# A streaming encoder step: the sample's convolution taps as ScalarE products, summed in groups on VectorE

## The reference

```
u      = ga_in * sigmoid(gb_in)                       # GLU, 512 channels
u_full = concatenate([past_conv, u])                  # 30 frames of history in front, zeros for the prompt
c      = depthwise causal convolution of u_full, 31 taps, one weight per channel and tap
c      = silu(layernorm(c + conv_dw_b))
conv_out = c @ w_conv_out
x = x + (sigmoid(ga) * attn_out + sigmoid(gc) * conv_out) @ w_out
```

## Time and profile before

| what | value |
|---|---|
| median of 3 runs | 1997.33 us (1996.92 to 1998.19) |
| profiled execution | 1996.86 us, span 1995.1 us |
| PE busy in the span | 1872.1 us (94%) |
| DVE busy | 1094.6 us (55%) |
| ACT busy | 766.1 us (38%) |
| POOL busy | 261.0 us (13%) |
| mean granted PE clock | 0.979 of full speed |

### The profile page before, as it was taken

How to read it: one execution, slowest core, us unless ns; L and a number is a source line. 1 busy time by engine, 2 the same in 40 slices (tenths; PEclk the granted TensorE clock), 3 DMA queues, 4 the chain that set the end, 5 groups by cost and what they waited for, 6 DMA issues and landing times.

```text
span 1995.1 us, 28433 instructions
## 1 busy us (share of the span) xinstructions
PE 1872.1 (94%) x11088; PEld 1647.4 (83%) x11088; DVE 1094.6 (55%) x1712; ACT 766.1 (38%) x1471; POOL 261.0 (13%) x287
## 2 busy tenths in 40 slices
PE   6977999999989966988999999999999999999998
PEld 3533799899989944656988889999999999999997
DVE  1045799897988977776454343333443333433333
ACT  2235655622367147765122233333223333333321
POOL 1001122122296022330000000000000000000000
PEclk9988999999999988999999999999999999999999
DMA  7110110332121323775321133333433333433332
GB/s 210 17 54 18 46 43 27 107 102 91 62 66 44 99 89 109 267 249 215 137 111 43 32 147 126 127 125 124 162 114 122 121 122 123 157 125 126 126 126 105
DMA packets 74236, 220.28 MB, mean 110 GB/s; under 512 B 14197, under 2 KB 25109, under 8 KB 65315
## 3 DMA queue, kind: packets, MB, share of 16 engines
q1 hardware_dynamic: 67963, 205.05, 30.3%
q10 hardware_dynamic: 6192, 14.16, 1.8%
HBM read 197.26 MB, written 21.89 MB: 110 GB/s over the span
## 4 chain that ended last, share of the span: by engine, by line
PE 56%; ACT 2%; DVE 1%; issue 1%; DVEq 0%; ACTq 0%
PE ps L653 17%; PE ps L652 17%; PE ps L651 17%; PE ps L881 1%; PE ps L858 1%; ACT buf L1260 1%; PE ps L915 1%; PE ps L900 1%; PE ps L871 1%; DVE buf L1571 1%; PE ps L971 0%; PE ps L887 0%; DVE buf L1396 0%; ACT buf L1250 0%; ACT buf L1302 0%
## 5 line engine op out<-in xcount | busy, mean ns | idle before, releaser
L651 PE MATMUL ps<-buf,buf 128*128 128x384 f32 (+2 forms) x2364 | 830.7, 351 | 17.3 <-DVE buf L1396 11.7
L653 PE MATMUL ps<-buf,buf 128*128 128x384 f32 (+2 forms) x2364 | 832.6, 352 | 0.0
L652 PE MATMUL ps<-buf,buf 128*128 128x384 f32 (+2 forms) x2364 | 830.7, 351 | 0.0
L651 PEld LDWEIGHTS ps<-buf,buf 128*128 128x128 f32 x2364 | 446.6, 189 | 43.2 <-DVE buf L1396 10.0
L652 PEld LDWEIGHTS ps<-buf,buf 128*128 128x128 f32 x2364 | 446.5, 189 | 24.3
L653 PEld LDWEIGHTS ps<-buf,buf 128*128 128x128 f32 x2364 | 446.2, 189 | 24.3
L1396 DVE TENSOR_TENSOR buf<-buf,buf 128x1024 fp32r<-128x1024 f32 (+4 forms) x245 | 335.6, 1376 | 184.2 <-ACT buf L1374 39.1
L1744 DVE TENSOR_TENSOR buf<-buf,ps 128x384 f32<-128x384 f32 x66 | 36.5, 553 | 403.1 <-PE ps L653 403.1
L1519 DVE SCALAR_TENSOR_TENSOR buf<-buf,buf,buf 128x1024 f32<-128x1024 f32 x240 | 197.4, 864 | 4.0
L1372 ACT ACTIVATE buf<-ps 128x384 f32<-128x384 f32 x66 | 32.5, 492 | 295.9 <-PE ps L653 295.9
L1374 ACT ACTIVATE buf<-buf 128x384 fp32r<-128x384 f32 x66 | 34.7, 525 | 282.1 <-DVE buf L1744 282.1
(11 more groups left out here) (182 smaller groups left out, 1746.5 us busy)
## 6 DMA issues: line engine op xcount, KB each, us to landing
buf<-in_w_ffn SPq DMA_DIRECT2D x67, 1024.0 KB, 5.6
buf<-in_w_ffn SPq DMA_DIRECT2D x66, 512.0 KB, 3.6
buf<-in_cache_k SPq DMA_DIRECT2D x16, 1024.0 KB, 7.3
buf<-in_cache_v SPq DMA_DIRECT2D x16, 1024.0 KB, 10.5
buf<-in_w_cols SPq DMA_DIRECT2D x24, 512.0 KB, 4.1
buf<-in_x SPq DMA_DIRECT2D x18, 512.0 KB, 3.7
gate_scr<-buf ACTq DMA_DIRECT2D x16, 576.0 KB, 4.8
buf<-gate_scr SPq DMA_DIRECT2D x16, 576.0 KB, 5.2
```

The source lines that it names most:

```text
L651: mm(dst, whi, xhi, start=start, stop=False)
L652: mm(dst, whi, xlo, start=False, stop=False)
L653: return mm(dst, wlo, xhi, start=False, stop=stop)
```

## The change

The prompt's part of a tap stays on DVE. The sample's part becomes a product alone, made by ACT into a buffer `prod` of two halves with six slots each, in the free bytes at `o_gmix`: group n of tile j holds 6 taps (the first group, with the bias in tap 0) or 5, six groups per tile, 24 in all. DVE adds up each group with one reduction over the slots (`sample_sum`, reading slot after slot, 128 floats apart) and adds that to the running sum of the tile; the last add of a tile goes straight to `cT`. ACT makes groups 0 to 5 behind named evacuations of the gate columns, groups 6 to 20 at the end of named turns of the head loop, the last three behind it. ACT waits until the half it writes has been summed; DVE waits until the group it sums is made.

The order of DVE's stream is written anew: after every tap a group sum where the tap's number is 8, 13, ... 118, the `qkv_low` behind taps 20, 50, 66, 82, 98 and 114, the memset behind 118, the last group sum at the end. The copy to `cT` takes the prompt's 1024 columns alone. PE's `layer_sums` also waits for the 24 sums. Two semaphores are merged into others (`biasS_in` into `near_in`, `rik_made` into `rstd_made`), and SP no longer waits for `conv_made` in front of `qkv_in(3)`.

```diff
+        prod = take(12 * P, o_gmix).rearrange("p (e d t) -> p e d t", e=2, d=6)
+        cuts = (0, 6, 11, 16, 21, 26, CK)
+        NPART = len(cuts) - 1
...
             qkv_in(2)
-            sp.wait_ge(S("conv_made"), 2)
             sp.wait_ge(S("out_state"), 48)
...
                     pe.wait_ge(S("conv_made"), CT)
+                    pe.wait_ge(S("sample_summed"), CT * NPART)
...
+            def sample_products(n):
+
+                j, i = divmod(n, NPART)
+                if n >= 2:
+                    act.wait_ge(S("sample_summed"), n - 1)
+                else:
+                    act.wait_ge(S("mask_made"), NSEL)
+                for d in range(cuts[i], cuts[i + 1]):
+                    out = prod[:, n % 2, d - cuts[i]].rearrange("p (s q) -> p s q", s=NS)
+                    x = uSamp[:, j, :, d:d + QS]
+                    if d:
+                        l = ac(out, x, ACT.Copy, scale=cw[:, j, d:d + 1])
+                    else:
+                        l = ac(out, x, ACT.Identity, scale=cw[:, j, d:d + 1], bias=cb[:, j:j + 1])
+                    l.then_inc(S("sample_made"), 1)
+
+            in_columns = {(20, 2): 0, (21, 1): 1, (21, 2): 2, (22, 2): 3, (23, 1): 4, (23, 2): 5}
+            in_heads = {13 * k // 5: 6 + k for k in range(15)}
...
                     l.then_inc(S("col_evac"), 1)
+                    if (t, c) in in_columns:
+                        sample_products(in_columns[t, c])
...
                     qkv_high(q // NT + 1)
+                if q in in_heads:
+                    sample_products(in_heads[q])
             qkv_high(5)
+            for n in range(6 + len(in_heads), CT * NPART):
+                sample_products(n)
...
             def conv_tap(j, d):
 
-                outs = (acc[:, 0:NP], acc[:, NP:NTOK].rearrange("p (s q) -> p s q", s=NS))
-                w = cw[:, j, d:d + 1]
-                for x, out in ((uT[:, j, d:d + NP], outs[0]), (uSamp[:, j, :, d:d + QS], outs[1])):
-                    if d == 0:
-                        ch.add(ve.tensor_scalar(out, x, w, cb[:, j:j + 1], ALU.mult, ALU.add))
-                    else:
-                        ch.add(ve.scalar_tensor_tensor(out, x, w, out, ALU.mult, ALU.add))
-                ch.wait()
+                x, w, out = uT[:, j, d:d + NP], cw[:, j, d:d + 1], acc[:, 0:NP]
+                if d == 0:
+                    ch.link(ve.tensor_scalar(out, x, w, cb[:, j:j + 1], ALU.mult, ALU.add))
+                else:
+                    ch.link(ve.scalar_tensor_tensor(out, x, w, out, ALU.mult, ALU.add))
                 if d == CK - 1:
-                    ve.tensor_copy(cT[:, j], acc).then_inc(S("conv_made"), 1)
+                    ve.tensor_copy(cT[:, j, 0:NP], out).then_inc(S("conv_made"), 1)
                     dve.wait_ge(S("conv_made"), j + 1)
 
+            def sample_sum(n):
+
+                j, i = divmod(n, NPART)
+                dve.wait_ge(S("sample_made"), j * CK + cuts[i + 1])
+                src = prod[:, n % 2, 0:cuts[i + 1] - cuts[i]].rearrange("p d t -> p t d")
+                total, part = acc[:, NP:NTOK], newneg
+                if n:
+                    dve.wait_ge(S("sample_summed"), n)
+                if i == 0:
+                    l = ve.tensor_reduce(total, src, AX.X, ALU.add)
+                else:
+                    ch.link(ve.tensor_reduce(part, src, AX.X, ALU.add))
+                    dst = cT[:, j, NP:NTOK] if i == NPART - 1 else total
+                    l = ve.tensor_tensor(dst, total, part, ALU.add)
+                l.then_inc(S("sample_summed"), 1)
...
-            convolve(20)
-            qkv_low(0)
-            convolve(20)
-            for f in range(1, 6):
-                qkv_low(f)
-                convolve(14)
-            dve.wait_ge(S("qn_made"), 2 * NT)
-            dve.wait_ge(S("turn_made"), NQK)
-            ve.memset(biasS, 0.0).then_inc(S("biasS_zero"), 1)
-            convolve(CT * CK)
+            sums = iter(range(CT * NPART))
+            low_behind = {20: 0, 50: 1, 66: 2, 82: 3, 98: 4, 114: 5}
+            for m, (j, d) in enumerate(all_taps, 1):
+                conv_tap(j, d)
+                if m >= 8 and m % 5 == 3 and m < 123:
+                    sample_sum(next(sums))
+                if m in low_behind:
+                    qkv_low(low_behind[m])
+                if m == 118:
+                    dve.wait_ge(S("qn_made"), 2 * NT)
+                    dve.wait_ge(S("turn_made"), NQK)
+                    ve.memset(biasS, 0.0).then_inc(S("biasS_zero"), 1)
+            for n in sums:
+                sample_sum(n)
```

More of the change, by code:

```diff
@@ L527, in _ @@
                 r = slice(h * QS, (h + 1) * QS)
-                sp.dma_start(biasS[r, PAST - P:PAST], skewed(h)[0:QS, 0:P]).then_inc(S("biasS_in"), 16)
+                sp.dma_start(biasS[r, PAST - P:PAST], skewed(h)[0:QS, 0:P]).then_inc(S("near_in"), 16)
                 sp.dma_start(biasS[r, PAST:LS].rearrange("p (s q) -> p s q", s=NS),
                              skewed(h)[0:QS, P:P + QS].unsqueeze(1).to_broadcast([QS, NS, QS]))\
-                    .then_inc(S("biasS_in"), 16)
+                    .then_inc(S("near_in"), 16)
             def keys_in(st_):
@@ L1422, in _ @@
             ve.tensor_reduce(ssq[:, 0:NT], ikn[:, :, 0:HD], AX.X, ALU.add).then_inc(S("ssik_made"), 1)
-            dve.wait_ge(S("rik_made"), 1)
+            dve.wait_ge(S("rstd_made"), NT + 1)
             ch.link(ve.tensor_tensor(ikwN[:, :, 0:HD], ikwN[:, :, 0:HD],
@@ L1706, in normed @@
             def normed(t):
-                dve.wait_ge(S("rstd_made"), NT + t + 1)
+                dve.wait_ge(S("rstd_made"), NT + t + 2)
                 ve.scalar_tensor_tensor(xs[:, t % 2], x1[:, t], rstd[:, t % 3:t % 3 + 1], gmix, ALU.mult, ALU.mult)\
@@ L1801, in _ @@
             ch.link(gp.tensor_scalar(msq[:, 0:NT], ssq[:, 0:NT], 1.0 / HD, EPS, ALU.mult, ALU.add))
-            gp.tensor_tensor(rsq[:, 0:NT], msq[:, 0:NT], mhalf[:, 0:NT], ALU.pow).then_inc(S("rik_made"), 1)
+            gp.tensor_tensor(rsq[:, 0:NT], msq[:, 0:NT], mhalf[:, 0:NT], ALU.pow).then_inc(S("rstd_made"), 1)
             for b in range(2, PB):
@@ L1859, in _ @@
             pool.wait_ge(S("qkv_done"), NQ)
-            pool.wait_ge(S("near_in"), 16 * H)
-            pool.wait_ge(S("biasS_in"), 16 * 2 * H)
+            pool.wait_ge(S("near_in"), 16 * 3 * H)
             for i in range(len(steps)):
```

## The result

The changed kernel takes 2008.55 us (median of 4 runs, 2007.56 to 2008.69) against 1997.12 for the kernel before beside it (1995.99 to 1998.19): ratio 1.0056, 95% interval 1.0039 to 1.0074. It is slower, by some 11 us. The forecast was 1996.3, no change; the time lies inside its range of 1988 to 2012, near the 2011 of the slower rival.

What follows compares the result with a forecast made beforehand. Attention's start bounds: the later of DVE's convolution (709.0) and PE's q/k/v plus first logits. It moves to 710.2, +1.2; clock -2.2; net -1.0 against 1996.86 gives 1995.9, and 0.47 for the median gives 1996.3; range 1988 to 2012.

Steps and rivals of the forecast that it cites:

- the slower rival: In DVE's group sums, the strided reduction takes two steps per element; attention starts 14 us later, total near 2011; chance 0.28.
- DVE's work: In the convolution, 124 sample parts (32.2 us) go and 24 group sums (28 us) come, so only 4 us less.
- DVE waits for the first group: After 8 taps, at 483 to 485, DVE stands 8 to 10 us until ACT makes group 0 at 493.0.
- split 1 ends at: DVE's weight subtraction qkv_low(1), needed by PE's block 1, ends at 569.2; PE wanted it at 558.65.
- I take the row of line 1422, the only reduction there is: DVE's group sums priced from 0.755 us for 576 elements: 0.82 us for 5 products, 0.96 for 6.
- The prediction's own sign of being wrong: Reductions above 1.3 us, PE not idle ahead of block 1, or DVE's copy still the last thing before attention.
- The bound from the other side: If an element 512 bytes from the last costs two steps, each reduction is 0.67 us longer, 16 over all sums.
- The chain of waits: DVE waits 8 to 10 us for group 0, PE about 10.5 before block 1, and PE becomes last before attention.
- 0.17 and 0.035 us of gaps: Per group sum on DVE: 0.17 us for the reduction's three semaphore waits, 0.035 for the gap of the add.
- the term: PE's q/k/v work after split 1, from 569.2 to 708, including POOL's gains and some 2 us of lower clock.
- the gain of 2.2 us: PE's lower clock around 712 goes: 1.15 us on line 841 and about as much on two groups before it.
- The drop around 712: PE's lower granted clock after its 10.87 us idle before attention; forecast to go, since PE no longer stands there long.

Runs made afterwards that it cites:

- with neighbours: The changed kernel with a group's products stored side by side, ACT writing with a step of 24 bytes and DVE summing neighbours: 2001.54 us, ratio 1.0026.
- the two with one repair: The changed kernel with products stored side by side (2001.54 us), and the changed kernel with ACT's first six groups behind earlier evacuations (1996.86 us).
- changed, first groups earlier: The changed kernel with ACT's first six product groups behind earlier evacuations, (19,1) to (22,2) in place of (20,2) to (23,2): 1996.86 us, ratio 1.000.
- changed, both: The changed kernel with products side by side and ACT's first six groups behind earlier evacuations, splits as changed: 1994.93 us, ratio 0.9991.

## Why the prediction was wrong

The numbers are those of the profiled executions; the last column is the changed kernel with neighbouring products, where the forecast's price of the reduction holds.

| step | forecast | after | with neighbours |
|---|---|---|---|
| reduction of 640, of 768 (us) | 0.82, 0.96 | 1.31, 1.54 | 0.82, 0.95 |
| DVE's work | -4 | -0.3 | -10.2 |
| DVE waits for the first group | 8 to 10 | 8.6 | 9.0 |
| split 1 ends at | 569.2 | 571.5 | 566.8 |
| PE waits for it | 10.5 | 12.8 | 5.4 |
| PE's last projection | 708 | 714.3 | 708.7 |
| DVE ends the convolution | 700 | 706.5 | 697.2 |
| attention starts | 710.2 | 717.2 | 711.6 |
| attention's length | -2.2 | +3.7 | -0.8 |
| median (us) | 1996.3 | 2008.55 | 2001.54 |

The profile with neighbours began the stage 1.2 us earlier than the kernel before (first tap 471.84), which has to be added to its times of day when they are held against the forecast. The attention of that one profile is the shortest but one of all, and the median of the same kernel lies 3.9 us above that execution.

**The step that failed** is "I take the row of line 1422, the only reduction there is". That row reads neighbours, so it could not speak against the slower rival; the new reductions read with a step of 512 bytes, and take 0.49 and 0.585 us more. The prediction's own sign of being wrong came, reductions above 1.3 us. With that one price repaired 6 of the 11 us come back, so it is half of the loss and not all of it.

The bound from the other side was worked out and then not taken; its size (two steps per element, 0.67) was its author's own and too high by a third. That the rival's 2011 still came near is in part luck: it has PE done at 723, which was 714.3, and attention shorter by 2.2 us, where it was 3.7 longer.

**The chain of waits was right:** the first group's wait, PE standing in front of block 1, the change of places between DVE and PE at attention's start, and the full clock between 705 and 717. With the price of the reduction repaired, the end of split 1, the ends of PE and DVE and the start of attention lie within 3 us of the forecast, though not for the reasons given each time, and PE's wait is half of the forecast one: I put 0.17 and 0.035 us of gaps on every sum, and the repaired run shows that DVE's work falls by 10 and not by 4; but PE is then held by POOL (8.0 us in place of 5.1) and by the low clock behind its wait, and ends where it was forecast to. Two errors met there. In the changed kernel too the gaps hid a part of the slow sums: nine of them ahead of split 1 cost 4.6 us more than forecast, and split 1 was only 2.3 late.

**PE's end was short by 6 us for two reasons.** The wait was 2.3 longer. And what follows the wait was taken for 138.8 us (569.2 to 708); it is 142.8 in the changed kernel and 141.9 to 142.7 in the two with one repair. The kernel before needs 139.7 for it: the term was put below what the row of the kernel before gives (558.65 to 698.38), and 2.8 us of low clock came on top.

**The clock in attention** was the second failed step: the gain of 2.2 us is in neither profile of the changed kernel, which show +3.7 and +1.9, and in the first it makes 5.9 of the 12.8 us that lie between forecast and profile. The drop around 712 did go, as forecast, but the clock falls again some microseconds into attention (721.1 to 724.5 and 731.3 to 734.7 in the first profile). The gain was taken from eight matmuls of line 841 and not from the stage. Over the thirteen profiles the stage takes 220.7 to 225.3 us: 220.7 to 224.4 in the five with the old convolution, 220.8 to 225.3 in the eight with the new one. The two ranges overlap; that the change slows attention is not shown, and what sets the clock's falls there stays open.

**How much each cause bears.** The slow sums and the first wait both stand in front of split 1; by the ratios the repair of the one gives back some 6 us, of the other 11, and of both 13. The first wait was in the forecast and is no error of it. The 13 are less than the two together, since from then on PE's own work sets the start of attention: at best 698.4 + 2.9 = 701.3. And of what is left to win there, the kernel before gets as much from its splits alone. The table holds the stage by itself, free of where it begins in each profile:

| kernel | first tap | attention starts | between |
|---|---|---|---|
| before | 473.0 | 709.0 | 236.0 |
| changed | 473.2 | 717.2 | 244.0 |
| changed, neighbours | 471.8 | 711.6 | 239.8 |
| changed, first groups earlier | 473.8 | 709.3 | 235.5 |
| changed, both | 473.6 | 707.1 | 233.5 |
| changed, both, splits 1 and 2 earlier | 471.1 | 703.8 | 232.7 |
| before, splits where the change has them | 472.5 | 708.6 | 236.1 |
| before, splits behind 46 to 110 | 471.9 | 703.2 | 231.2 |

The other edits of the change (the merged semaphores, the load that SP no longer holds back) are in all the repaired runs as well, which lose nothing against the kernel before once the first groups come early; no part of the loss is seen to be theirs.

## What to carry to other kernels

Before moving work off the engine that ends last, ask whether it is last by its work or by its waits: here 11.7 us of idle time in the middle made DVE last. Moving five instructions a few taps later gained 4 us; taking 124 operations away lost 11, and gained 2 to 3 with all that was repaired. A reduction is priced from a row with the same step between the elements it sums; store what will be summed as neighbours, since ACT's scattered writes were hidden here and DVE's scattered reads were not. Where two engines feed each other in fixed order through a buffer of two halves, count what stands behind each wait in both streams, for a third instruction may be caught between them.

## What the runs showed of the hardware that was not expected

- A reduction over a step of 16 bytes or more (16, 36, 256, 512 measured) costs 1.17 to 1.27 us for 576 to 640 elements against 0.75 to 0.82 at 4 and 8 bytes: 0.63 to 0.74 ns more for each element, and not a second full step of 1.05. In the working kernel it is 0.08 us more still (1.31), which no run here takes apart.
- ACT's product writing with a step of 24 bytes takes 557 ns in the mean against 436 when it writes floats side by side, but its 120 products keep ACT busy for 41.8 against 39.0 us: most of the longer time runs alongside the next product.
- Around PE's wait for split 1 the granted clock was at its lower level, 1.2 GHz, for 17.1 us where the wait was 12.84, for 10.2 with 5.68 and 5.35, for 3.4 with 2.75, and not at all with 1.71.
